# The opening of a two-layer transformer kernel: modulation made in quarters, first feature tiles and their products moved ahead of the last quarter

## The reference, cut to what matters

```python
mod   = split(silu(c)     @ w_mod[0] + b_mod[0], 6)    # for the 256 latent tokens: sh1, sc1, ga1, ...
mod_c = split(silu(c_ctx) @ w_mod[0] + b_mod[0], 6)    # for the 256 context tokens
h  = rmsnorm(x,  g_pre_mix) * (1 + sc1)  + sh1
hc = rmsnorm(xc, g_pre_mix) * (1 + sc1c) + sh1c
u  = h @ w_in ;  uc = hc @ w_in
```

## Time and profile before

| | |
|---|---|
| median of three runs | 1396.09 us |
| the profiled execution's own time | 1395.11 us |
| its span, first to last instruction | 1393.3 us |
| granted clock of TensorE, mean | 0.999 |
| PE busy | 98% of the span |
| DVE, ACT, POOL busy | 72%, 49%, 6% |
| HBM read | 238.75 MB |

### The profile page before, as it was taken

One profiled execution on the slowest core, in us unless ns is written; L12 is line 12 of the kernel. 1 busy time (PEld: TensorE's weight loads), 2 busy tenths in 40 slices (PEclk: granted clock), 3 DMA queues, 4 the chain that ended last, 5 costly groups with the idle time before them and its releaser, 6 DMA issues.

```text
span 1393.3 us, 21170 instructions
## 1 busy us (share of the span) xinstructions
PE 1366.2 (98%) x8250; PEld 1172.7 (84%) x8250; DVE 1010.1 (72%) x1544; ACT 688.0 (49%) x1096; POOL 83.7 (6%) x125
## 2 busy tenths in 40 slices
PE   6999999999999999999999999999999999999997
PEld 4888667988888888889877888989998889899996
DVE  3768686686876757678986765677996557886867
ACT  4531466650422304566466554566445674654544
POOL 0000000100101011000000630000000000000000
PEclk9999999999999999999999999999999999999999
DMA  9522650453636658345313655555454444445453
GB/s 382 209 74 78 231 223 1 152 196 122 246 135 236 213 169 302 118 160 199 121 47 133 207 187 198 210 191 186 163 182 169 151 143 157 175 158 212 151 212 121
DMA packets 39509, 241.04 MB, mean 173 GB/s; under 512 B 4496, under 2 KB 4928, under 8 KB 15488
## 3 DMA queue, kind: packets, MB, share of 16 engines
q1 hardware_dynamic: 28624, 198.92, 39.4%
q0 software_dynamic: 10800, 40.92, 8.5%
HBM read 238.75 MB, written 1.07 MB: 172 GB/s over the span
## 4 chain that ended last, share of the span: by engine, by line
PE 88%; DVE 5%; ACT 3%; DMA 2%; issue 1%; SPq 0%; DVEq 0%; ACTq 0%
PE ps L756 36%; PE ps L856 19%; PE ps L889 5%; PE ps L779 5%; PE ps L811 3%; PE ps L782 2%; PE ps L720 2%; PE ps L951 2%; PE ps L919 2%; PE ps L1206 1%; PE ps L1394 1%; DMA w<-in_stream 1%; PE ps L1378 1%; PE ps L1020 1%; DMA U<-in_start 1%
## 5 line engine op out<-in xcount | busy, mean ns | idle before, releaser
L756 PE MATMUL ps<-h_both,w_hi 128*128 128x256 f32 (+1 forms) x2336 | 447.9, 315 | 0.4 <-issue 0.3
L536 DVE TENSOR_TENSOR w_lo<-w,w_hi 128x1024 fp32r<-128x1024 f32 x332 | 393.0, 1228 | 55.9 <-ACT w_hi L526 51.7
L526 ACT ACTIVATE w_hi<-w 128x1024 fp32r<-128x1024 f32 x332 | 331.9, 1052 | 205.2 <-DMA w<-in_stream 205.0
L756 PEld LDWEIGHTS ps<-h_both,w_hi 128*128 128x128 f32 x2336 | 360.7, 191 | 31.3 <-issue 4.4
L756 PE MATMUL ps<-h_both,w_lo 128*128 128x256 f32 (+1 forms) x1168 | 285.9, 314 | 0.0
L756 PEld LDWEIGHTS ps<-h_both,w_lo 128*128 128x128 f32 x1168 | 197.8, 191 | 13.1
L856 PE MATMUL ps<-w_hi,g_hi 128*128 128x512 f32 x344 | 134.7, 392 | 2.1 <-DVE g_lo L3261 0.7
L856 PE MATMUL ps<-w_hi,g_lo 128*128 128x512 f32 x344 | 134.1, 390 | 0.0
L856 PE MATMUL ps<-w_lo,g_hi 128*128 128x512 f32 x344 | 121.0, 390 | 0.0
L779 PE MATMUL ps<-h_both,w_hi 128*128 128x512 f32 x288 | 88.2, 398 | 0.0
L856 PEld LDWEIGHTS ps<-w_hi,g_hi 128*128 128x128 f32 x344 | 64.6, 188 | 17.2 <-DVE g_lo L3261 2.1
(11 more groups left out here) (376 smaller groups left out, 1976.6 us busy)
## 6 DMA issues: line engine op xcount, KB each, us to landing
w<-in_stream SPq DMA_DIRECT2D x176, 1024.0 KB, 4.8
hf<-in_mod_blocks POOLq DMA_DIRECT2D x38, 512.0 KB, 3.8
SW<-in_mod_blocks POOLq DMA_DIRECT2D x18, 512.0 KB, 5.0
U<-in_start SPq DMA_DIRECT2D x4, 1024.0 KB, 15.1
GA<-gates POOLq DMA_DIRECT2D x6, 512.0 KB, 4.5
w<-in_start SPq DMA_DIRECT2D x2, 1024.0 KB, 7.7
w<-in_stream SPq DMA_DIRECT2D x4, 512.0 KB, 9.9
GA<-in_start SPq DMA_DIRECT2D x2, 1024.0 KB, 14.1
```

Of the source, the lines that this page charges most:

```text
L526: act.activation(k.w_hi[:, c.slot, half], k.w[:, c.slot, half], ACT.Copy).then_inc(k.hi_done, 1)
L536: dve.tensor_tensor(k.w_lo[:, c.slot, half], k.w[:, c.slot, half], k.w_hi[:, c.slot, half].bitcast(f32), ALU.subtract).then_inc(k.lo_done, 1)
L756: last = pe.matmul(k.banks(2 * c.pair, n, j * (512 if tiles == 2 else n)), w[a][:, c.slot, at:at + 128], h[b][:, kt * stride:kt * stride + n],
```

## The change

The modulation of the first half (chunks 0 to 3) is made in quarters instead of halves: shift 0, scale 0, shift 1, scale 1, each of 256 columns with a copy, two transposes and a sum of its own. The tiles kt 0 and 1 of the latent tokens, and their products with the first weight chunk, are put between the third quarter's rows and the fourth's. SP issues chunk 2 before chunk 1, and half 0 of the first weight chunk right behind chunk 2. Two products without a reader are left of three. Behind the context tokens' products, the second weight chunk's products with kt 0 to 3 for j = 0 come ahead of the rows of chunks 6 and 7, and those for j = 1 ahead of the transpose of kt 7. The last load of the opening waits for three rows' counts instead of one.

```diff
-START_CHUNKS = 8
+START_ORDER = 0, 2, 1, 3, 4, 5, 6, 7
+START_QUARTERS = 4
...
-OCCUPIED, OCCUPIED_FIRST = 2, 3
+OCCUPIED, OCCUPIED_FIRST = 2, 2
...
-    for n in range(START_CHUNKS):
+    for n in START_ORDER:
         if n >= 6:
             sp.wait_ge(start_in(k, n), 16)
         sp.dma_start(start_chunk(k, n), t["start"][n]).then_inc(start_in(k, n), 16)
+        if n == 2:
+            sp.dma_start(k.w[:, 0, 0:HALF], t["stream"][0][:, 0:HALF]).then_inc(k.w_loaded[0], 16)
         if n == 3:
-            sp.dma_start(k.w[:, 0, 0:HALF], t["stream"][0][:, 0:HALF]).then_inc(k.w_loaded[0], 16)
...
-    sp.wait_ge(k.s("start_mm"), 1)
+    sp.wait_ge(k.s("start_mm"), 3)
...
+def quarter_rows(k, pe, sec, quarter, bank):
+    chunk = 2 * sec + quarter
+    pe.wait_ge(start_in(k, chunk), 16)
+    for kt in range(KT):
+        g = kt % 4
+        last = pe.matmul(k.banks(bank, 256, 0, slice(32 * g, 32 * g + 32)), k.cond[:, kt * 32:kt * 32 + 32],
+                         start_chunk(k, chunk)[:, kt * 256:kt * 256 + 256], start=kt < 4, stop=kt >= 4)
+    last.then_inc(k.s("start_mm"), 1)
+def quarter_features(k, pe, sec, quarter, bank):
+    pe.wait_ge(k.s("start_copy"), 2 * quarter + sec + 1)
+    for kt in range(2):
+        at = sec * 512 + quarter * 256 + kt * 128
+        last = pe.transpose(k.banks(bank, 128, kt * 128), k.start_rows[:, at:at + 128], k.C[:, C_IDENT:C_IDENT + 128])
+    last.then_inc(k.s("mod_mm"), 1)
...
     pe.wait_ge(k.s("cond"), 1)
+    quarter_rows(k, pe, 0, 0, 3)
+    quarter_rows(k, pe, 1, 0, 7)
+    pe.wait_ge(k.s("consts_in"), 16)
+    quarter_features(k, pe, 0, 0, 3)
+    for kt in range(3):
+        pe_transposed(k, pe, kt, x_tiles)
+    quarter_features(k, pe, 1, 0, 7)
+    quarter_rows(k, pe, 0, 1, 2)
     for j in range(2):
-        start_rows(k, pe, 0, j, 3)
...
+        contraction_tokens(k, pe, first, h, 0, j, x_ready, (0, 1))
+    pe.wait_ge(k.s("mod_read"), 2)
+    pe_transposed(k, pe, 3, x_tiles)
+    quarter_features(k, pe, 0, 1, 2)
+    quarter_rows(k, pe, 1, 1, 3)
+    quarter_features(k, pe, 1, 1, 3)
+    pe.wait_ge(k.s("mod_read"), 3)
     for _ in range(OCCUPIED_FIRST):
         pe.matmul(k.banks(2, 512), k.C[:, C_IDENT:C_IDENT + 128], k.Y[:, 0, 0:512], start=True, stop=True)
     for j in range(2):
-        contraction_tokens(k, pe, first, h, 0, j, x_ready)
+        contraction_tokens(k, pe, first, h, 0, j, x_ready, (2, 3))
...
     for j in range(2):
         contraction_tokens(k, pe, first, h, 1, j, ready)
+    contraction_half(k, pe, second, h, 0, (0,))
     pe.wait_ge(k.s("hf", "mix0"), 8)
     for j in range(2):
         start_rows(k, pe, 6, j, 7)
     for kt in range(4, 7):
         pe_transposed(k, pe, kt, all_tiles)
     start_features(k, pe, 7, 7)
-    contraction_half(k, pe, second, h, 0, (0,))
+    contraction_half(k, pe, second, h, 0, (1,))
     pe.wait_ge(k.s("mod_read"), START_STEPS)
     pe_transposed(k, pe, 7, all_tiles)
-    contraction_half(k, pe, second, h, 0, (1,))
...
-    rows(0, 3)
-    rows(2, 7)
+    quarter(0, 0, 3)
+    quarter(1, 0, 7)
     feed_hi(k, act, first, (0,))
-    features(0, range(4))
+    features(1, range(2))
+    quarter(0, 1, 2)
+    quarter(1, 1, 3)
+    features(2, range(2, 4))
     act.wait_ge(k.s("ctx_in"), 16)
     act_stats(k, act, o, (2, 3))
...
-    modulation(1, 3)
-    modulation(3, 3)
+    quarter(0, 0, 3)
+    quarter(1, 0, 7)
     feed_lo(k, dve, first, (0,))
-    for n in range(4):
+    for n in range(2):
+        dve_features(k, dve, o, n)
+    quarter(0, 1, 2)
+    quarter(1, 1, 3)
+    for n in range(2, 4):
         dve_features(k, dve, o, n)
     dve_tokens(k, dve, o, (2, 3))
```

More of the change, by code:

```diff
@@ L139, in mod_mm_count @@
 def mod_mm_count(n):
-    return sum(kind != "rows" for kind, *_ in MOD_STEPS[:n])
+    return sum(kind != "rows" for kind, *_ in MOD_STEPS[:n]) + START_QUARTERS // 2
 def mod_vec_count(n):
@@ L1182, in start_rows @@
         last.then_inc(k.s("start_mm"), 1)
+def quarter_rows(k, pe, sec, quarter, bank):
[12 more added lines that the diff above has]
+    last.then_inc(k.s("mod_mm"), 1)
 def start_features(k, pe, n, bank):
-    pe.wait_ge(k.s("start_copy"), n // 2 + 1)
+    pe.wait_ge(k.s("start_copy"), n // 2 + 1 + START_QUARTERS // 2)
     pe.wait_ge(k.s("mod_read"), n - 1)
@@ L1210, in contraction_half, with contraction_tokens @@
         last.then_inc(k.chunk_mm, 1)
-def contraction_tokens(k, pe, c, h, tokens, j, ahead):
+def contraction_tokens(k, pe, c, h, tokens, j, ahead, kts=range(4)):
     w = {"hi": k.w_hi, "lo": k.w_lo}
-    for kt in range(4):
+    for kt in kts:
         if j == 0 and kt == 0:
@@ L1242, in pe_start @@
     pe.wait_ge(k.s("cond"), 1)
-    for j in range(2):
-        start_rows(k, pe, 0, j, 3)
[L1245 to L1253, removed]
+    quarter_rows(k, pe, 0, 0, 3)
[6 more added lines that the diff above has]
+    quarter_rows(k, pe, 0, 1, 2)
+    for j in range(2):
+        contraction_tokens(k, pe, first, h, 0, j, x_ready, (0, 1))
[5 more added lines that the diff above has]
+    pe.wait_ge(k.s("mod_read"), 3)
     for _ in range(OCCUPIED_FIRST):
@@ L1787, in rows, with quarter, features @@
         at = n // 2 % 2 * 512
-        act.wait_ge(k.s("start_mm"), n // 2 + 1)
+        act.wait_ge(k.s("start_mm"), n // 2 + 1 + START_QUARTERS // 2)
         act.activation(k.start_rows[:, at:at + 512], k.banks(bank, 512), ACT.Copy).then_inc(k.s("start_copy"), 1)
-    def features(part, steps):
-        act.wait_ge(k.s("start_gain"), part + 1)
+    def quarter(sec, part, bank):
+        at = sec * 512 + part * 256
+        act.wait_ge(k.s("start_mm"), 2 * part + sec + 1)
+        act.activation(k.start_rows[:, at:at + 256], k.banks(bank, 256), ACT.Copy).then_inc(k.s("start_copy"), 1)
+    def features(gains, steps):
+        act.wait_ge(k.s("start_gain"), gains)
         for n in steps:
@@ L1806, in act_start @@
     rows(4, 3)
-    features(0, range(4, 8))
+    features(2, range(4, 8))
     feed_hi(k, act, first, (1,))
@@ L1811, in act_start @@
     feed_hi(k, act, first + 1, (1,))
-    features(1, range(8, 12))
+    features(3, range(8, 12))
 ROWS_IN = {"mix2": 32, "ffn": 64}
@@ L2672, in modulation, with quarter @@
                                      ALU.mult).then_inc(k.s("start_gain"), 1)
+    def quarter(sec, part, bank):
+        at = feature(0, sec) + part * 4
+        of = k.mod[:, at:at + 4].rearrange("p (k v) -> p k v", v=2)
+        each = lambda column: col(k, column + part * 2, 2).unsqueeze(2).broadcast_to([128, 2, 2])
+        groups = k.banks(bank, 256).rearrange("p (k g n) -> p k n g", k=2, g=4)[:, :, 0:2, :]
+        dve.wait_ge(k.s("mod_mm"), 2 * part + sec + 1)
+        dve.tensor_reduce(of, groups, AX.X, ALU.add).then_inc(k.s("mod_read"), 1)
+        dve.wait_ge(k.s("mod_read"), 2 * part + sec + 1)
+        o.link(dve.tensor_tensor(of, of, each(FC["b_mod", 0] + sec * KT), ALU.add))
+        if sec in GAIN_SECTIONS:
+            dve.scalar_tensor_tensor(of, of, 1.0, each(FC[GAIN_SECTIONS[sec], 0]), ALU.add,
+                                     ALU.mult).then_inc(k.s("start_gain"), 1)
     first = At(FIRST["win", 0])
     dve_tokens(k, dve, o, (0, 1))
-    modulation(1, 3)
-    modulation(3, 3)
+    quarter(0, 0, 3)
+    quarter(1, 0, 7)
     feed_lo(k, dve, first, (0,))
-    for n in range(4):
+    for n in range(2):
[3 more added lines that the diff above has]
+    for n in range(2, 4):
         dve_features(k, dve, o, n)
```

## The result

| | before | changed |
|---|---|---|
| median of nine runs | 1395.67 us (1394.97 to 1396.48) | 1399.63 us (1399.02 to 1401.23) |
| ratio | | 1.0031, 95% interval 1.0022 to 1.0040 |
| span of the profiled execution | 1393.3 us | 1397.7 us |

A forecast was written before the change was run, and what follows sets the result against it. PE, busy 98% of the span, bounds the kernel. 1.05 + 0.5 + 2.73 - 0.21 - 0.53 = +3.5 us on the profiled 1395.11 gives 1398.6; the median's 1.0 more makes 1399.6 us, range 1397.0 to 1402.0.

The forecast's parts named there:

- Latent tiles early: Front of the opening: PE's first latent product at 18.3 us against 21.52, a gain of 3.2 us.
- Second gain late: Front: last modulation quarter's gain stands at 23.1, so ACT starts kt 2 at 23.15, 1.7 us later.
- Context tokens 1.05 later: Context stage: the 1.7 us delay shrinks to 1.05; PE's first context product at 30.4 instead of 29.34.
- Wait for w_lo 0.5: Behind the context products: PE waits 0.5 us for DVE's second w_lo, ready at 34.9.
- Twelve products 2.73: End of the opening: second weight chunk's twelve products, ahead of rows 6 and 7, take 2.73 us, up to 37.7.
- Rows of chunks 6 and 7: End of the opening: 1.72 us instead of 1.93 as a 0.21 wait goes; done at 39.4, 4.1 later.
- Cover and chain at the end, net -0.53: Behind rows 6 and 7: fixed-length chain; of 2.73 taken out, 2.2 return as PE's waits for tiles.
- Sum: Whole opening: the terms add up to +3.5 us; PE ends it at 57.5 instead of 54.0.
- The front is as quick as before: Rival, 24%: full-speed transposes leave kt 2 only 0.6 late, slack absorbs it; only the end's +2.5 remains, 1398.6 us.
- The clock stays low: Rival, 15%: PE idles between 16.3 and 24.5 and runs at half speed there; sum +5.8, 1401.9 us.
- The new order of loads does not arrive: Rival, 4%: scale 0 lands at 13.9 as before, first stretch up to 2.5 later; +5.6, 1401.7 us.
- Faster: Rival, 7%: early tiles pull the front ahead, twelve products fill PE's wait for chunk 7; -0.8, 1395.3 us.

The follow-up runs named there:

- e2: The changed kernel with the end of PE's order put back as before; 1396.34 us, 0.9 above the kernel before, ratio 1.0009.
- e3: As e2, with the last quarter's rows and the transposes ahead of them put before the first products; 1395.68 us, ratio 1.0003.
- e1: The kernel before, with only the end of PE's order as in the changed kernel; 1398.38 us, ratio 1.0023.
- e5: The changed kernel with the last weight half put behind the tiles on ACT and DVE; 1398.39 us, 2.8 above the kernel before.
- e8: The changed kernel without the front's two products that nobody reads; 1400.90 us, 5.3 above the kernel before.
- e7: e2 with chunks 0, 1, 2, 3 and then the weight half loaded in the old order; 1400.03 us, 4.5 above the kernel before.
- e4: e3 with six of the second weight chunk's j = 0 products between the rows of chunks 6 and 7; 1396.44 us.
- e6: e3 and e5 in one, with three products in front of chunk 7's rows; 1395.29 us, ratio 1.0000.

## Why the prediction was right

- **Latent tiles early.** Expected first product 18.3, measured 18.11. The estimate that no row showed, transposes at half speed up to 15.3, held in this execution: six in 1.49 us. It doesn't hold in each: e2 and e3 had them at full speed. In e2 that moves the first product and kt 2 by 1.1 us, and chunk 4's late landing takes it up. That the profiled execution bore the estimate out was luck.
- **Second gain late.** Kt 2 on ACT expected 23.15, measured 23.11, which is 1.65 behind the kernel before. By e2 and e3, the place of the rows gives 1.33 of what can be moved here, and the transposes' half speed 1.07.
- **Context tokens 1.05 later.** First product expected 30.4, measured 30.27 (29.34 before): 0.93. The size came out, the path did not. I had PE waiting until 28.5 for DVE's scaling, with the copy of chunk 5's rows no longer in the way; but the transposes start at 28.24, and the copy still stands right in front of the first context tile (28.28, 28.77). What shrinks 1.65 to 0.92 is that PE has six products fewer to make between the rows of chunks 4 and 5 (2.62 for 3.35).
- **Wait for w_lo 0.5.** Measured 0.50 by the bracket, in e1 0.49.
- **Twelve products 2.73.** From their first to the rows behind them they take 2.95 (34.83 to 37.78): I left out that the first three and the last three issue in some 0.8 instead of 0.68.
- **Rows of chunks 6 and 7.** Expected to end at 39.4, they end at 39.7. The term of -0.21 was wrong: I took the wait of 0.21 in the earlier trace rows for time that would go. But the rows last 1.93 us with it and 1.93 us without it (37.78). The weight loads had waited while PE still had products in hand; it was never on the path.
- **Cover and chain at the end, net -0.53.** Waits expected 2.2 in all; by the starts of the tiles they are 0.97 + 0.30 + 0.55 + 0.39 = 2.2, and the net is -0.52 (from the rows' end to the end of the opening 57.94 - 39.65 = 18.29 us, before 54.02 - 35.21 = 18.81). e1 shows them without the front, e5 shortens them by shortening the chain.
- **Sum.** +3.5 expected, 3.92 in the opening. Of the difference, the wait that was none gives 0.21 and the products' length 0.22; the context tokens take 0.12 back, and the rest is under 0.1. The median moved by 4.0. I set the sum on the median of the first three runs of before (1396.09, nine give 1395.67), and by luck this made the forecast meet the measured 1399.63 more closely than its sum did.
- **Rivals.** "The front is as quick as before" is half there in e2's profile: kt 2 is 0.58 late, as this rival had it, but chunk 4's late landing then sets the pace. "The clock stays low" did not happen in the change and does in e8. I had sized a product without a reader at 0.43, which is one of its two instructions; three of them take 2.40, 0.80 each. So the idle piece that I had at 1.5 us in front of 24.5 was 0.40 long, and without the two products, in e8, it is 2.16. "The new order of loads does not arrive" is refuted by 11.32 and by e7. "Faster" needed a front 2 us early; it was late. Its other half, products in PE's wait for chunk 7, was tried on e3's front, which is 0.7 early: six of them cost time (e4), and three of them together with e5's shorter chain can't be told from no difference (e6). (Its terms add up to -0.7, not -0.8.)

What is open: the runs of the kernels with quarters scatter more than those before (e2: seven of eleven at 1395.7 to 1396.4, four at 1397.4 to 1398.3). The longest executions of most kernels are also those with a lower mean granted clock: 0.998 for three of e2's four and for the changed kernel's three longest (1400.84 to 1401.23), 0.999 or 1.000 in the other executions of these two, and 0.998 in e8's profiled execution, which shows the fall. A stretch like e8's in some executions would fit both; no such execution of the other kernels was profiled, so this is not shown. In two profiles chunks landed later than in the others with no other order of issue: by 1.4 us in e2 (chunk 4), by 0.9 to 1.6 in e4. Why they land late I did not find.

## What to carry to other kernels

Work pulled ahead in an in-order engine (one that works its program off in the order written) pushes back whatever stands behind it: ask which later chain starts there (here the last quarter's rows), and put the start of the longest chain first. Independent products are worth most behind the step that starts a long chain through other engines, as its cover; in front of it they cost their full length, and a wait for the chain comes on top. When a front is sped up, look for the transfer that lands last in it before counting a gain. And when a run's median comes out as expected, look whether its profile got there by the expected path: here e2's did not.

## What the runs showed of the hardware that was not expected

- TensorE went to its lower level behind an idle piece of 2.16 us (e8): the granted clock was 1.00 for the first 0.7 us of work after it and then 0.50 for some 3.3 us. It did not go down behind 1.63, 0.50 and 0.40 us in the changed kernel, nor behind 1.26 us in e2. Two products of 128 x 512 whose result nobody reads kept it up; they were worth 1.4 us.
- The time at which it rises at the start is not fixed: the transposes from 13.4 us ran at half speed in the changed kernel and e5 (six in 1.49 and 1.45 us), at full speed in e2 and e3 (0.82), with the same instructions before them. The granted clock reads 1.00 in both.
